# Two-layer hybrid encoder on one core: moving the banded half's output projection, projections in steps of three token tiles, and other banks for the memory's keys and values

## The reference

```python
def token_mixer(h, ...):                    # h: rms-normed x
    qa, ka, va, qb, kb, vb = split(h @ w_in)
    oa = rms_norm(banded_attention(rope(qa), rope(ka), va, 128, S, sink))      # 8 heads of 64
    ob = rms_norm(dilated_mixture(rope(qb), rope(kb), vb))                      # 8 heads of 64
    return concatenate([oa, ob]) @ w_out

def cross_attention(h, mem, ...):           # 4 heads of 128 on 256 memory rows
    q = h @ w_cq ; k, v = split(rms_norm(mem, g_mem) @ w_ckv)
    return softmax(q k^T / sqrt(128)) v @ w_co

for l in range(2):
    x = x + token_mixer(rms_norm(x, g_mix[l]), ...)
    x = x + cross_attention(rms_norm(x, g_cross[l]), mem, ...)
    x = x + conv_ffn(rms_norm(x, g_ffn[l]), ...)          # 1024 -> 2*2816 -> 1024
return rms_norm(x, g_final)
```

## Time and profile before

| | |
|---|---|
| Runs | 2363.2, 2363.51, 2364.24 us |
| Profiled execution | 2367.2 us, its span 2365.4 us, mean granted TensorE clock 0.972 |
| TensorE busy | 2226.2 us (94%) |
| VectorE, ScalarE, GpSimd busy | 1117.8 us (47%), 628.2 us (27%), 781.5 us (33%) |
| DMA | 145.11 MB, 61 GB/s over the span |

### The profile page before, as it was taken

The page is one execution under the profiler, slowest core; times in us unless marked ns, Lnnn a source line. Parts: engine busy times, 40 slices in busy tenths (PEclk is TensorE's granted clock), DMA queues, the critical chain, the costliest instruction groups (busy, mean ns, idle before and its releaser), DMA issues. The chain is left out here.

```text
span 2365.4 us, 39034 instructions
## 1 busy us (share of the span) xinstructions
PE 2226.2 (94%) x13528; PEld 1948.3 (82%) x13528; DVE 1117.8 (47%) x2157; ACT 628.2 (27%) x1556; POOL 781.5 (33%) x436
## 2 busy tenths in 40 slices
PE   7999988999899999999999999889999999999996
PEld 7888967778788888888798888778787888888885
DVE  3575645516555144425355656444265541552353
ACT  3445444124311001001044554432343110110001
POOL 2211202342244444444432111023423444444442
PEclk9999979999999999999999999799999999999998
DMA  5100011220111211111231000121111112112122
GB/s 214 63 19 28 28 45 54 90 71 28 46 63 62 71 62 61 64 62 62 64 143 37 23 31 30 36 99 63 63 32 51 62 62 64 62 62 71 62 62 80
DMA packets 40286, 145.11 MB, mean 61 GB/s; under 512 B 4688, under 2 KB 4944, under 8 KB 39888
## 3 DMA queue, kind: packets, MB, share of 16 engines
q1 hardware_dynamic: 32832, 117.45, 15.2%
q10 hardware_dynamic: 7312, 25.78, 3.0%
HBM read 133.78 MB, written 9.44 MB: 61 GB/s over the span
## 5 line engine op out<-in xcount | busy, mean ns | idle before, releaser
L732 POOL CAST w_hi<-w_landed_tile 128x1024 fp32r<-128x1024 f32 x216 | 225.3, 1043 | 1535.6 <-PE ps L773 1525.4
L773 PE MATMUL ps<-x_turned,w_hi 128*128 128x512 f32 (+1 forms) x3072 | 668.8, 340 | 3.8 <-DVEq L1341 2.1
L773 PEld LDWEIGHTS ps<-x_turned,w_hi 128*128 128x128 f32 x3072 | 524.7, 188 | 107.8 <-issue 4.0
L734 POOL TENSOR_TENSOR w_lo<-w_landed_tile,w_hi 128x1024 fp32r<-128x1024 f32 x216 | 556.0, 2574 | 17.3
L773 PE MATMUL ps<-w_hi,x_turned 128*128 128x256 f32 (+1 forms) x2304 | 550.9, 323 | 10.5 <-ACT scratch L1198 5.0
L773 PEld LDWEIGHTS ps<-w_hi,x_turned 128*128 128x128 f32 x2304 | 396.9, 195 | 37.3 <-ACT rows L1233 6.6
L773 PE MATMUL ps<-x_turned,w_lo 128*128 128x512 f32 (+1 forms) x1536 | 395.0, 339 | 0.0
L773 PE MATMUL ps<-w_hi,regions 128*128 128x512 f32 (+1 forms) x1312 | 375.1, 369 | 0.0
L773 PE MATMUL ps<-w_lo,x_turned 128*128 128x256 f32 (+1 forms) x1152 | 363.1, 315 | 0.0
L773 PEld LDWEIGHTS ps<-w_hi,regions 128*128 128x128 f32 x1312 | 238.9, 188 | 41.8 <-DVE regions L1441 0.3
L1248 ACT ACTIVATE scratch<-scratch 128x768 f32<-128x768 f32 x44 | 37.3, 848 | 840.3 <-DVE scratch L1511 840.3
(11 more groups left out here) (90 smaller groups left out, 2089.7 us busy)
## 6 DMA issues: line engine op xcount, KB each, us to landing
w_landed_tile<-weights_dram SPq DMA_DIRECT2D x216, 512.0 KB, 3.4
x_hbm<-x_residual ACTq DMA_DIRECT2D x2, 3072.0 KB, 15.4
x_residual<-x_hbm ACTq DMA_DIRECT2D x4, 1536.0 KB, 7.8
rows<-mem_in_dram ACTq DMA_DIRECT2D x8, 512.0 KB, 4.3
scratch<-mem_in_dram ACTq DMA_DIRECT2D x8, 512.0 KB, 5.4
x_residual<-x_in_dram SPq DMA_DIRECT2D x6, 512.0 KB, 5.8
out<-scratch ACTq DMA_DIRECT2D x6, 512.0 KB, 2.7
gain<-gains_dram ACTq DMA_DIRECT2D x3, 512.0 KB, 16.2
```

Source lines behind the costliest of these rows:

```text
L732: nc.gpsimd.tensor_copy(W_HI[:, s, :], W_IN[:, s, :]).then_inc(w_rounded, 1)
L734: nc.gpsimd.tensor_tensor(W_LO[:, s, :], W_IN[:, s, :], W_HI[:, s, :].bitcast(F32), ALU.subtract).then_inc(w_split, 1)
L773: ins = pe.matmul(dst, lhsT, rhs, start=start, stop=stop, skip_group_check=True)
```

## The change

- Beside B1, all eight turns of the banded half now go into steps 1 and 2 (before: spread over steps 1 to 4), and `outa` starts in step 3 instead of step 4. Its other side items are woven through all later steps: the loads of three memory tiles come with the second `outa` item, the turns k = 4 and 5 follow, the three scalings of memory rows go to steps 7 to 9, the squares of the first dilated half come last.
- `out` and `co` take three token tiles per item instead of six. Turns that stood in groups of four (for two k) are placed one or two at a time between these items, in `out` for c = 0 and c = 1 and partly in `co`. The adds of three tiles follow their item. The six `part` additions go from between the two column halves to just before the last `out` items of c = 1.
- Memory values use banks 0 to 3, one per split, instead of banks 1, 2, 0, 1. Memory keys use banks 4, 5, 2, 3 instead of 1, 2, 1, 2.
- Three `crossq` items of head 2 (`AHEAD = 3`) stand before the first cross scores.

```diff
@@ beside_last_stage
     out = [[item] for k in range(KD // 2) for item in turn_items("out", k)] + [[("unspill", 0)]]
-    half = first_half_out()
-    late = [[item] for k in (KD // 2, KD // 2 + 1) for item in turn_items("out", k)]
-    late += [[("memload", b, TURNED) for b in range(3)]] + [[("square", "ob0", t)] for t in range(NT)]
-    late += [[("scale", "mem", b)] for b in range(3)]
-    return out + half[:4] + weave_steps(half[4:], late)
+    late = [[("memload", b, TURNED) for b in range(3)]]
+    late += [[item] for k in (KD // 2, KD // 2 + 1) for item in turn_items("out", k)]
+    late += [[("scale", "mem", b)] for b in range(3)] + [[("square", "ob0", t)] for t in range(NT)]
+    return out, weave_steps(first_half_out(), late)
@@ plan_layer
-    beside = beside_last_stage()
-    items += weave(steps[b:b + 2], third[-2:] + beside[:4])
-    items += weave(steps[b + 2:], beside[4:])
+    turned, beside = beside_last_stage()
+    items += weave(steps[b:b + 2], third[-2:] + turned)
+    items += weave(steps[b + 2:], beside)
...
-    items += turn[0] + turn[1] + [("out", 0, 4)] + turn_items("out", 6) + turn_items("out", 7)
-    items += [("rstd", "ob"), ("unspill", 1), ("memload", 3, TURNED), ("out", 0, 5)] + turn[2]
-    items += [("scale", "mem", 3), ("out", 0, 6)] + turn[3] + [("out", 0, 7)]
-    items += [("add", "out", 0, t) for t in range(NT)] + [("part", t) for t in range(NT)]
-
-    items += [("out", 1, 4), ("out", 1, 5)] + turn_items("cross", 0) + turn_items("cross", 1)
-    items += [("out", 1, 6)] + turn_items("cross", 2) + turn_items("cross", 3) + [("out", 1, 7)]
-    items += [("add", "out", 1, t) for t in range(NT)]
+    beside = [turn_items("out", 6), turn_items("out", 7) + [("rstd", "ob"), ("unspill", 1), ("memload", 3, TURNED)]]
+    beside += [[turn[2]], [turn[3]], [turn[4], ("scale", "mem", 3)], [turn[5]], [turn[6]], [turn[7]]]
+    items += turn[:2]
+    for step, (k, half) in zip(beside, product(range(KD // 2, KD), range(2))):
+        items += [("out", 0, k, half)]
+        if k == KD - 1:
+            items += [("add", "out", 0, t) for t in range(3 * half, 3 * half + 3)]
+        items += step
+    turn = [[]] + [turn_items("cross", k) for k in range(4)] + [[("part", t) for t in range(NT)]]
+    for step, (k, half) in zip(turn + [[]] * 2, product(range(KD // 2, KD), range(2))):
+        items += [("out", 1, k, half)]
+        if k == KD - 1:
+            items += [("add", "out", 1, t) for t in range(3 * half, 3 * half + 3)]
+        items += step
...
-    items += flat(q[:2 * KD])
-    items += weave(steps[:2 * NT - 1], q[2 * KD:])
+    items += flat(q[:2 * KD + AHEAD])
+    items += weave(steps[:2 * NT - 1], q[2 * KD + AHEAD:])
...
+    for c in range(2):
+        for i, (k, half) in enumerate(product(range(HX // 2, HX), range(2))):
+            items += [("co", c, k, half)]
+            if k == HX - 1:
+                items += [("add", "co", c, t) for t in range(3 * half, 3 * half + 3)]
+            if c and i:
+                items += turn_items("ffn", i - 1)
...
+KEY_BANKS = (4, 5, 2, 3)
@@ banks_of
-        return [(1 + it[1] % 2, ("split", "kx", it[1]))]
+        return [(KEY_BANKS[it[1]], ("split", "kx", it[1]))]
-        return [((HX + 2 * it[1] + i) % 3, ("split", "vx", 2 * it[1] + i)) for i in range(2)]
+        return [(2 * it[1] + i, ("split", "vx", 2 * it[1] + i)) for i in range(2)]
@@ TensorE, kind in ("out", "co")
-                    for t in range(NT):
+                    for t in range(3 * half, 3 * half + 3):
```

36 lines of the change are left out of this document (17 added, 19 removed).

## The result

The changed kernel takes 2303.62 us (median of 4 runs, 2302.24 to 2305.95) against 2363.74 us (4 runs, 2363.2 to 2364.24): ratio 0.9751, 95% interval 0.9734 to 0.9768, so 60 us less, 30 per layer. The forecast was 2315, range 2303 to 2338. The profiled execution took 2302.74 us, span 2301.0, at a mean granted clock of 0.983 (before: 2367.2, 2365.4 and 0.972).

The account below looks back on a forecast made before the run. TensorE, busy 94% of the span, was taken as the bound, with only its gaps and clock to win. Terms summed to 25.8 us per layer, 24.3 after small waits, 48.6 for both layers: 2315 us, range 2303 to 2338.

Parts of the forecast that it names:

- (a): Front of the second dilated stage: outa starts 8.2 us earlier, net gain 4.7 us per layer, bounds -3.4 and +11.9.
- (c): End of the second dilated stage: the 4.67 us wait shrinks to 0.4 and half clock goes, +6.9 us, bounds +2.5 and +8.
- (f): Six additions moved before the adds of c = 1: TensorE waits for the first add, -0.6 us, at worst -4.5.
- (h): Three cross-query items before the first cross scores: wait of 1.97 and clock drop go, +3.4 us, between +0.5 and +3.7.
- (b): Inside the second dilated stage: two waits on a keep and two on turns, 4.46 us against 3.50, -1.0, between -2 and 0.
- (c) to (f): Memory turns to memory values, including projection and cross turns spread between matmul groups: 14.05 us gain per layer.
- (g): New banks for the memory's keys: idle of 1.40 and 1.90 us goes, +3.3 us per layer.
- (i): co: one of two groups of four turns is cut, +1.34 us per layer.
- rival 1: The gaps go but the clock does not follow: 14 us per layer after small waits, 2335 us; chance 0.18.
- The 1.5 per layer for small waits: Deduction for five small waits of 0.2 to 0.4 us behind other engines where TensorE arrives earlier.
- Rival 2: Moved scalings and additions each meet a GpSimd split that holds VectorE: about 6 us per layer, 2327 us; chance 0.14.
- Rivals 3 and 4: Half clock through the whole second dilated stage, 2433 us, chance 0.03; moved work hidden either way, within 0.2%, chance 0.04.

Follow-up runs that it names:

- f1_spread: Changed kernel with the sixteen banded turns again beside four attention steps of the second dilated stage and outa from step 4: 2310.81 us.
- f3_parts: Changed kernel with the six additions of the cross half's sums back behind the additions of c = 0: 2303.97 us.
- e4_halves: Kernel before with only out and co in steps of three token tiles, turns and additions between them: 2342.15 us, ratio 0.9908.
- e1_banks: Kernel before with only the other banks for memory values and keys: 2352.87 us, ratio 0.9963.
- e2_ahead: Kernel before with only three cross-query items placed before the first cross scores: 2355.13 us, ratio 0.9973.
- g1_early: Changed kernel with the first eight banded turns moved beside the third stage and outa from step 1 of the second dilated stage: 2292.10 us.
- h1_all: g1_early with early turns one product apart, three outa items before the first values, and fourth-chunk feed-forward turns behind the first gate and up product: 2310.19 us.
- h3_apart: g1_early with early turns one product apart and the feed-forward turns moved, but no outa items pulled ahead: 2286.71 us, ratio to before 0.9679.
- h4_seams: h1_all with three empty places added to the list beside the second dilated stage: 2278.74 us, ratio to before 0.9645.
- f2_scales: Changed kernel with the first three memory scalings again behind the squares, at the end of the second dilated stage: 2312.35 us.

## Why the prediction held, step by step

The mechanism was right in the large terms: the waits went where the forecast said, and the clock followed. The size was 11 us short (2315 against 2303.6), and the result lies only 0.6 us inside the lower end of the range. That end does not follow from the terms: with (a) and (c) at their better ends the sum is 24.3 + 7.2 + 1.1 = 32.6 per layer, 2298, not the 2303 that I wrote; the worse ends of (f) and (h) give some 2328, not 2326. So the range held by a narrow margin. By the prediction's own steps:

- (a) Front: in layer 2 the forecast positions were met within 0.2 us up to `outa`, which came 8.7 and 8.3 us earlier in the two layers against 8.2. f1_spread showed that the gain is the shorter time at half clock. The clock rose some 2 us sooner behind `outa` than in the kernel before: by the single products of the timeline 1.8 us behind its start (0.78, 0.63, then 0.39 from 1464.45), where the kernel before still shows 0.63 at 1509.83, 3.1 us behind, and 0.40 from 1510.85. Two us less at half clock are worth 1.
- (b) Inside the stage: mis-sized, with (a) the largest miss. I had four waits, 2 x 1.17 and 2 x 1.06, 4.46 together. Both waits of 1.06 came (1.06, 1.07), those on a `keep` were 0.19 and 0.89: 3.21 together. Whether one costs depends on what ScalarE has before it and how much work TensorE has, which I had not worked out per place. Together (a) and (b) gave 7.0 and 6.3 instead of 3.7; in layer 2 the 1.25 of waits and the 1 of clock are most of the 2.6.
- (c) to (f), from the memory turns to the memory values: 13.1 and 15.1 against 14.05. Right as a sum, and (c)'s remaining 0.4 of waiting was 0.47. Term (f) was wrong in sign: no wait appeared, and the old place meets a split (f3_parts). The wait of 0.6 is real where the old banks are kept: e4_halves has one of 0.53 on an addition before the memory values, which start there in bank 1. In the whole change they start in bank 0, whose addition is the first to end.
- (g) Banks: 5.6 and 4.0 against 3.3. The idle went as forecast. The rest is 0.7 that the two waits cost beyond their idle and, in layer 1, 1.6 of a half clock that other traces with the same waits do not have (e1_banks).
- (h) and (i): 3.7 against 3.4, with the reserve that the clock's part of (h) is not in every trace (e2_ahead); 1.1 against 1.34 in layer 1. In layer 2 (i) was lost to a dip of the clock at 1703, behind turns that had waited 0.70 and 0.67. g1_early has the same dip in both layers, h1_all, h3_apart and h4_seams in one of theirs, the other traces in none: no long gap stands before it, against what I had held against rival 1. The feed-forward wait of 1.34 is 1.60 now; placing those turns behind the first gate and up product took it to 0.54.
- The 1.5 per layer for small waits appeared nowhere: 3 us of the 11. (a) and (b) are 6 of it, (g) 3, and (i) takes nearly 2 back.

Rival 1 (gaps go, the clock stays) is refuted by the windows. Rival 2, VectorE held by GpSimd, is the interesting one. It names a real mechanism, seen in f2_scales and f3_parts as in the earlier trace rows, and the change gains from avoiding it: of the moved scalings and additions only the first scaling of a layer overlaps a split, and since it begins first, the split is held and not the scaling (1.36 and 3.23 us). The Trainium skill ("GPSIMD Engine Reference", section Specifications) says that GpSimd shares its SBUF interfaces with VectorE and collides with its instructions that have two SBUF inputs; the rows of f2_scales agree. Read strictly, the rule spoke against moving them; it should be read with the time of each split beside the time of each such instruction, and with which of the two begins first. Rivals 3 and 4 had no trace in the result.

## What to carry to other kernels

Where one engine is the bound, judge a place by what stands between the last product into a bank and the next product that wants it: the emptying instruction starts when its own engine's queue lets it, and the filler must cover that whole queue. In these runs shifting a list by a few places cost 23 us (h1_all against h3_apart) or won 31 (h4_seams against h1_all) with every instruction the same. Before moving a VectorE instruction with two SBUF inputs, look at whether a GpSimd instruction runs in its new place, and which of the two begins first. Idle and clock have to be measured in the same windows, of more than one trace or layer: at the front of the stage clock was most of the difference (5.2 us against 1.2 of idle in f1_spread), while behind a single wait of 1.97 us it was 1.5 us in six cases and nothing in two.

## What the runs showed of the hardware that I had not expected

- The collision is all or nothing by its size: a VectorE scaling begun just behind a split ended 1.08 and 1.07 us behind the split's end, as if it had stood still meanwhile (3.39 and 3.18 us instead of 1.28). Of six additions beside a split one was held (2.04 us for 0.68), not all slowed.
- It is held the other way round when VectorE begins first: the scaling begun 0.36 us before a split took 1.36, and the split 3.23 instead of 2.4, in both layers of the changed kernel. In these traces the order of the two starts decides which engine pays, and GpSimd had time to spare there: it stood idle for 2.85 us behind that split.
- The last gap of g1_early, 3.72 us, was followed by some 7 us of half clock with dense products behind it (0.52 from 1445 to 1452), while a gap of 2.54 among turns in the changed kernel stood in a stretch that was mostly low until `outa` (30 us at 0.72, which is 16.8 us at the lower level, 1.8 of them behind `outa`'s start).
- The same wait is followed by half clock in one layer and not in the other, in one and the same execution: 1.97 us before the first cross scores in six of eight cases, 1.90 us before a memory key in two of eight. Such stretches are probably a part of what makes single runs of one kernel differ; no run isolates them.
